# A two-block hybrid layer stack: SBUF tensors begun on multiples of 128 bytes, and the grouped attention's values projected feature-major

## The reference

```
h = rms_norm(x, norm1_g);  proj = h @ w_in
y_a = mlstm(...);  y_b = gqa_branch(bq, bk, bv);  y_c = natten(...);  y_d = diff(...)
merged = sum over branches of sigmoid(gate) * (y @ w_up);  x = x + merged @ w_out
x = x + (silu(h2 @ w_ffn_gate) * (h2 @ w_ffn_up)) @ w_ffn_down
```

## The kernel before

| tensor | start | mod 128 | role |
|---|---|---|---|
| xn / xn_r, xn_hi | 1152, 17536 | 0, 0 | normalised x: full / low half, high half |
| raw, weights_hi, weights_lo | 33920, 50304, 58496 | 0 | weights |
| consts (2950 columns), cols (302 columns) | 66688, 78496 | 0, 32 | constants |
| y / y_r | 79712 | 96 | branch outputs; y_r also holds the low halves, and the feed-forward's and the entries' early high halves |
| x, x_again | 112480 | 96 | residual |
| first block: mixed / mixed_r, y_hi, gate | 128864, 145248, 178016 | 96 | merge and output projection |
| hidden / hidden_r, hidden_hi | 128896, 173952 | 0 | feed-forward, all three |
| layers: mixed / mixed_r, y_hi, gate | 137088, 153472, 186240 | 0 | merge and output projection |
| d_qk, d_v, lambda | 137088, 153472, 161664 | 0 | differential attention |
| distance_bias, b_qk, b_keys_twice, b_v, rotary_work, exps | 161696 and on | 32 | grouped attention and scores |

## Time and profile before

### The profile page before, as it was taken

One profiled execution on the slowest core, in us unless ns is written; L12 is line 12 of the kernel. 1 busy time (PEld: TensorE's weight loads), 2 busy tenths in 40 slices (PEclk: granted clock), 3 DMA queues, 4 the chain that ended last, 5 costly groups with the idle time before them and its releaser, 6 DMA issues. The chain is left out here.

```text
span 3963.5 us, 52449 instructions
## 1 busy us (share of the span) xinstructions
PE 3716.3 (94%) x20604; PEld 2886.7 (73%) x20604; DVE 2033.2 (51%) x3128; ACT 1536.4 (39%) x2414; POOL 399.1 (10%) x353
## 2 busy tenths in 40 slices
PE   7898889879999999999899999999899899999998
PEld 5456777658878887676667878887676677887887
DVE  4879565574443335636555443333636646443332
ACT  4454333543332233425453333223334554333222
POOL 0017233000011110410000001100010000001100
PEclk9899989979999999999999999999999999999999
DMA  3011002103322232120212332233111112332222
GB/s 109 22 46 59 2 2 66 64 22 116 95 96 93 94 93 79 43 70 27 99 45 88 96 101 93 94 91 93 58 54 43 80 48 85 96 101 90 95 90 80
DMA packets 83488, 289.32 MB, mean 73 GB/s; under 512 B 9168, under 2 KB 9296, under 8 KB 82000
## 3 DMA queue, kind: packets, MB, share of 16 engines
q1 hardware_dynamic: 83136, 286.30, 22.3%
q10 hardware_dynamic: 144, 0.15, 0.0%
HBM read 284.32 MB, written 2.10 MB: 72 GB/s over the span
## 5 line engine op out<-in xcount | busy, mean ns | idle before, releaser
L473 DVE TENSOR_TENSOR weights_lo_r<-raw_weights,weights_hi_r 128x1024 fp32r<-128x1024 f32 (+2 forms) x554 | 637.0, 1150 | 1493.9 <-ACT weights_hi_r L467 1493.6
L467 ACT ACTIVATE weights_hi_r<-raw_weights 128x1024 fp32r<-128x1024 f32 (+2 forms) x554 | 547.2, 988 | 1640.8 <-PE ps L542 1583.6
L541 PE MATMUL ps<-xn_r,weights_hi_r 128*128 128x512 f32 x2672 | 1055.1, 395 | 0.0
L540 PE MATMUL ps<-xn_hi,weights_hi_r 128*128 128x512 f32 x1616 | 664.1, 411 | 41.4 <-DVE weights_lo_r L473 12.2
L542 PE MATMUL ps<-xn_hi,weights_lo_r 128*128 128x512 f32 x1616 | 639.2, 396 | 0.0
L541 PEld LDWEIGHTS ps<-xn_r,weights_hi_r 128*128 128x128 f32 x2672 | 508.3, 190 | 121.1 <-issue 11.0
L540 PE MATMUL ps<-y_r,weights_hi_r 128*128 128x512 f32 x1200 | 479.5, 400 | 6.9 <-DVE weights_lo_r L473 5.0
L542 PE MATMUL ps<-y_r,weights_lo_r 128*128 128x512 f32 x1200 | 476.8, 397 | 0.0
L540 PEld LDWEIGHTS ps<-xn_hi,weights_hi_r 128*128 128x128 f32 x1616 | 309.6, 192 | 134.3 <-issue 54.0
L542 PEld LDWEIGHTS ps<-xn_hi,weights_lo_r 128*128 128x128 f32 x1616 | 309.4, 191 | 67.4
L540 PEld LDWEIGHTS ps<-y_r,weights_hi_r 128*128 128x128 f32 x1200 | 225.7, 188 | 65.0 <-issue 11.7
(11 more groups left out here) (544 smaller groups left out, 5340.8 us busy)
## 6 DMA issues: line engine op xcount, KB each, us to landing
raw_weights<-in_w_ffn_dram SPq DMA_DIRECT2D x132, 512.0 KB, 3.7
raw_weights<-in_w_down_dram SPq DMA_DIRECT2D x48, 512.0 KB, 3.5
raw_weights<-in_w_out_dram SPq DMA_DIRECT2D x24, 512.0 KB, 3.6
bias_table<-in_window_bias_dram SPq DMA_DIRECT2D x8, 1280.0 KB, 10.1
raw_weights<-in_w_down_dram SPq DMA_DIRECT2D x24, 384.0 KB, 3.1
raw_weights<-in_w_hgrn_dram SPq DMA_DIRECT2D x16, 512.0 KB, 3.4
raw_weights<-in_w_mix_ssm_dram SPq DMA_DIRECT2D x16, 512.0 KB, 3.7
raw_weights<-in_w_a_qk_dram SPq DMA_DIRECT2D x16, 512.0 KB, 3.5
```

The costliest lines, as they stand in the source:

```text
L467: act.activation(self.k.w_hi[:, g % 2, 0:chunk.width], self.k.raw[:, slot, 0:chunk.width], ACT.Copy)\
L473: dve.tensor_tensor(self.k.w_lo[:, g % 2, 0:chunk.width], self.k.raw[:, slot, 0:chunk.width], self.k.w_hi[:, g % 2, 0:chunk.width].bitcast ...
L540: pe.matmul(out, w_hi, x_hi, start=start, stop=False)
L541: pe.matmul(out, w_hi, x_lo, start=False, stop=False)
```

## The change

Every tensor that is allocated on the left side of SBUF through `Kernel.sbuf` or `both_kinds`, and y_hi and hidden_hi, now begins on a multiple of 128 bytes: a filler tensor is allocated ahead of it where the next free address isn't one. Tensors allocated directly (xn_hi, raw_weights, consts, cols, x_again, norm_product) and those on the right side are allocated as before. With it y begins at 79744, x and x_again at 112512, the first block's mixed at 128896, hidden at 129024.

The values of the grouped attention become a sixth feature-major tile of their projection instead of a tokens job. In the next projection TensorE turns that tile with four transposes into PSUM bank 6 (after its first chunk), and ScalarE copies it to b_v after the root of the first rotary tile. TensorE's first turning matmul, which writes bank 6, waits for that copy.

```diff
+    def line_start(self, ctx):
+        at = (self.nc.sbuf_base + 31) // 32 * 32
+        if at % LINE:
+            self.made += 1
+            ctx.enter_context(self.nc.sbuf_tensor(f"to_line_{self.made}", [P, (LINE - at % LINE) // 4], F32))
     def sbuf(self, ctx, name, shape, side="left"):
+        if side == "left":
+            self.line_start(ctx)
     def both_kinds(self, ctx, name, shape):
+        self.line_start(ctx)
         at = (self.nc.sbuf_base + 31) // 32 * 32
...
 class Rotary(Nothing):
     def scalar(self, act):
...
             act.activation(self.rt[:, m % 2, :], bank(k.ps, 4 + m % 2), ACT.Sqrt,
...
+            if m == 0:
+                act.wait_ge(self.v_turned, 1)
+                act.activation(self.v_tok, bank(k.ps, 6).rearrange("p (j f) -> p j f", j=NT), ACT.Copy)\
+                    .then_inc(self.v_taken, 1)
     def tensor(self, pe):
         k = self.k
+        for j in range(NT):
+            mm = pe.transpose(k.ps[:, 6, j * P:(j + 1) * P], self.v[:, j * P:(j + 1) * P], k.const("ident"))
+        mm.then_inc(self.v_turned, 1)
         yield
...
             pe.wait_ge(self.normed, m + 1)
+            if m == 0:
+                pe.wait_ge(self.v_taken, 1)
...
 merge, feed_forward:
+        k.line_start(ctx)
         y_hi = ...        /        hidden_hi = ...
 layer_branches:
-            project(k, [(f"w_b_q{n}", b_qk[:, 0:4, :], 1.0), (f"w_b_k{n}", b_qk[:, 4:5, :], 1.0)], k.xn,
-                    tokens=(f"w_b_v{n}", b_v))
             with ExitStack() as work:
+                v = k.sbuf(work, "b_v_rows", [P, 1, T])
+                project(k, [(f"w_b_q{n}", b_qk[:, 0:4, :], 1.0), (f"w_b_k{n}", b_qk[:, 4:5, :], 1.0),
+                            (f"w_b_v{n}", v, 1.0)], k.xn)
...
                         beside=Together(DiffSetup(n, lam, slope),
-                                        Rotary(n, b_qk, b_k2, k.sbuf(work, "rotary_work", [P, 4, T]))))
+                                        Rotary(n, b_qk, b_k2, k.sbuf(work, "rotary_work", [P, 4, T]),
+                                               v[:, 0, :], b_v[:, :, :])))
```

More of the change, by code:

```diff
@@ L22 @@
 P = 128
+LINE = 128
 T = 512
@@ L3596, with __init__ @@
 class Rotary(Nothing):
-    def __init__(self, n, qk, k2, work):
-        self.n, self.qk, self.k2 = n, qk, k2
+    def __init__(self, n, qk, k2, work, v, v_tok):
+        self.n, self.qk, self.k2, self.v, self.v_tok = n, qk, k2, v, v_tok
         self.sq, self.rt = work[:, 0:2, :], work[:, 2:4, :]
@@ L3605, in open @@
         (self.squared, self.summed, self.root, self.inverse, self.normed, self.rotated, self.roped, self.doubled,
-         self.keys_ready) = semaphores(
-            k, ctx, "squared summed root inverse normed rotated roped doubled keys_ready")
+         self.keys_ready, self.v_turned, self.v_taken) = semaphores(
+            k, ctx, "squared summed root inverse normed rotated roped doubled keys_ready v_turned v_taken")
     def scalar(self, act):
```

## The result

The changed kernel takes 3938.45 us (median of 4 runs, 3935.38 to 3939.58), the kernel before on the same chip 3965.68 us (4 runs, 3964.38 to 3967.75). The ratio is 0.9927, its 95% interval [0.9915, 0.994]: 27.2 us faster, 13 less than the 40 forecast. The profiled span went from 3963.5 to 3936.6 us.

The account below looks back on a forecast made before the run. TensorE was taken to bound the kernel, its weight products by number of matmuls times pitch. Aligned starts, 30.5 us, and the values, 9.4 us, made some 40 us and a forecast of 3925 us, range 3913 to 3943.

Parts of the forecast that it names:

- Gate and up: Feed-forward gate and up products, three blocks: 3168 matmuls each 6.6 ns shorter once y_r is aligned, 20.9 us.
- rival B: Address counts, but merges and entries don't pass the gain on because TensorE waits there anyway: 3933 us, chance 0.08.
- hidden and the layers' y_hi and mixed stay on their multiples: Placement step: these tensors remain on multiples of 128 when y is raised, so no loss was counted for them.
- what the four have in common is where the moving operand begins: Reading of four earlier stages, two output projections, gate and up, down: start at 96 or 0 mod 128 sets pitch, 6.1 ns apart.
- part 1: Starts on multiples of 128 shorten matmuls in feed-forwards, entries, merges and first output projection: 30.5 us, all on TensorE's path.
- The layers' merges: Merges of the two layers, where only the low half y_r was unaligned: 64 dozens of matmuls, 3.3 us.
- The entries: Layers' gates and q/k from the early tiles: 432 matmuls reading y_r, each 6.1 to 6.6 ns shorter, 2.6 us.
- The second part: Grouped attention's values as a sixth feature-major tile: 5.4 us saved less 0.7 for transposes per layer, 9.4 us in sum.
- The tensors costed at nothing: Remaining aligned tensors, in plain float32 matmuls and elementwise work: at most 1 us, at least nothing, so not priced.
- Rival A: Address is not the cause of the slower pitch, so only the values' gain is left: 3956 us, chance 0.07 with Rival D.
- Rival C: Shorter values stage and added transposes keep the d projection at half clock, 60 to 75 us per layer: 4060 us, chance 0.03.
- Rival D: The change doesn't do what it says, tensors stay on 96: time as in Rival A, 1 in 100.

Follow-up runs that it names:

- the starts alone: The changed kernel with its starts on multiples of 128 but the grouped attention's values as in the kernel before: 3951.56 us, ratio to before 0.9964.
- the values alone: The changed kernel with its values' part but the start addresses of the kernel before: 3961.44 us, ratio to before 0.9985.
- first experiment: The changed kernel with all left-side tensors at 128 modulo 256 instead of on multiples of 128: 3932.76 us, ratio to before 0.9913; measured again 3930.91 us, 0.991.

## Why the prediction was right, and what in it was not

- **The direction and the place of most of the gain were right.** Gate and up gave 21.2 us where 20.9 were forecast. The time lies in the range, but 13 us above the forecast and 5 under the range's end, which had been set by rival B and a shift of the clock and not by what happened. That it holds is in part luck.
- **The step that failed** is "hidden and the layers' y_hi and mixed stay on their multiples", with the reading that led to it, "what the four have in common is where the moving operand begins". They stayed on multiples of 128, but they were 128 bytes away from the weights' phase afterwards. Of the stages in the earlier trace rows two were aligned, at 226.6 and 226.8 ns, and both stood at 128 modulo 256, as did the weights; a distance of 128 did not occur in them. They could not tell "multiple of 128" from "same phase as the weights". The text had hidden's new start, 129024, but read it modulo 128 only. It cost 8.8 us in the down projections and 1.9 in the layers' output projections.
- **A second step failed in part**: that all of part 1 is "on the path, since TensorE is the engine waited for". The layers' merges gave 0.3 us instead of 3.3. By the same cause as above their groups gained only 1.4 (the low half came into phase, the high half went out of it: 693.5 to 688.0 ns, in phase 681.8), and 1.1 of that was lost to longer steps elsewhere in the stage. The entries gave 1.1 instead of 2.6, though their groups gained 2.7. The first block's merge and output projection gave 2.0 and 0.95 for 2.5 and 1.2.
- **The second part** was forecast at 9.4 and gave 9.3 by its two places, 8.8 by the whole stretch: 6.54 us for 6.52, transposes 0.75 for 0.7, the copy and both waits hidden.
- **The sum.** From 39.9 the projections take 10.7, the merges 3.5, the entries 1.5 and the first output projection 0.25; gate and up add 0.3. That leaves 24.2. The remaining 2.6 or so of the 26.9 between the spans stand ahead of the merges, where the trace after has 17 us less at half clock; such time comes and goes between executions, so this part is probably chance.
- **The tensors costed at nothing.** The two plain float32 rows, 667 ns on b_keys_twice and 663 on d_qk, became 664 and 668, and VectorE's splits went from 684 and 683 to 685 and 684. In sum nothing moved, as forecast; but d_qk, on a multiple of 128 in both kernels, got 5 ns slower, so here too a multiple of 128 alone doesn't tell the time.
- **Rival A** (the address is not the cause) fell by the earlier trace rows against the windows after, and by the run with the starts alone. By the Trainium skill, SBUF — State Buffer, section "Specifications (TRN2)", SBUF has lines of 16 bytes. The prediction drew from this, as the rule against it, that part 1 would bring nothing. The runs don't agree with that inference: starts that are all multiples of 32 bytes give 680 to 703 ns.
- **Rival B** (merges and entries don't pass it on) was right for more than half: of the 8.4 us forecast for them 3.4 came. The first block's merge passed on 2.0 of its groups' 2.4, the layers' merges 0.3 of 1.4. Its time of 3933 is nearer to the result than the forecast's, though most of what the forecast lacked was lost elsewhere.
- **Rival C** did not come in its place: the clock of the d projections is no lower than before (0.95 and 0.97 before, 0.99 and 0.97 after). Over whole kernels the clock does move by a few us from version to version, as the values alone show. **Rival D** is out: the counts of starts moved with the addresses.
- **The observation that was set aside.** The text noted that dozens with an aligned high half lose 0.05 us and put it down as "somewhat uneven". This was a low half out of phase (693.5 ns), and the first sign that two tensors count, each by itself.
- **With the failed step mended** the forecast is nearer, and still too high. With everything in phase (first experiment) gate and up give 21.1 us, the down projections nothing, the first output projection 0.95 and the first merge 2.05. Taking what half clock cost out of the layers' merges and entries (an estimate: half of the time at half clock) leaves some 1.2 for the merges, and for the entries 1.2 at most is shown; with part 2's 8.8 to 9.3 this is 35 to 36. The measured gains of that version are 32.8 and 35.1 us, and by the estimate used above its runs lost 5.8 and 2.9 us more to the clock than the kernel before beside them.

Open: which two accesses meet. The trace shows that the pitch rises when moving operand and weights differ in phase, that one shifted buffer suffices, and that the costs don't add up by the number of passes; it does not show the mechanism. What makes the merges keep so little is open too. Starts other than multiples of 32 bytes, and moving operands of 128 columns, were not tried.

## What to carry to other kernels

Before aligning buffers, list every moving operand's and every weight buffer's start modulo 256 and bring the ones that meet in a matmul to the same value; a multiple of 128 allows two phases, and in this kernel the wrong one took 697 ns for 680. After any change to an allocation, follow the shift through all buffers behind it, for a speed that rested on a lucky address can be lost there. A few ns of pitch show up in a count of starts over 100 us or more, before they show in a kernel's time. Then compare the stage's length too: where TensorE waits now and then, as in the merges and entries, it keeps only a part of what its groups gain.

## What the runs showed of the hardware that was not expected

- The step from one fp32r matmul of 128x512 to the next is 226.7 ns when moving operand and weights begin at the same place modulo 256 bytes, and 229 to 234 ns on average when both halves are out of phase alike: up to 3.4%. The absolute place does not count between the two tried: all at 0 and all at 128 give the same 680 ns per group. The distance does not settle it to the last ns: at 128 the same stage of the same kernel took 699.9 ns in one execution and 697.2 in another.
- Distance 64 is cheaper than its neighbours (687 against 700) and 192, its mirror, is not (700), each in one stage of one execution. The cost is not symmetrical.
- At half clock the step is 427 ns in the kernel before, the version in phase and the one with the weights out of phase alike: there the placement shows no cost.
- The time at half clock (granted clock 0.50) in one profiled execution was between 223 and 282 us over kernels whose times differ by less than 2%. Runs of one kernel on one chip lay up to 13 us apart.
